# Two joined products for three in query heads 5 and 6 and in three units of the second attention's projection, and the third query tile's weight remainder made by VectorE

## What is computed

```python
def second_block(x, ...):
        xn = rmsnorm_2(h, norm1_g[layer])
        proj = xn @ w_in[layer]
        q_a, k_a, v_a, q_r, f_r, i_r, g_r = jnp.split(proj, IN_SPLITS, axis=-1)
        attn = moba_attention(q_a..., k_a..., v_a...)
        rec = hgrn2(q_r, f_r, i_r, g_r, lb_all[layer], rec_norm_g[layer])
        h = h + jnp.concatenate([attn, rec], axis=-1) @ w_out[layer]
        hn = rmsnorm_2(h, norm2_g[layer])
        h = h + peer_2(hn, ...)

def peer_2(x, wq, subkeys, u, v):
        qp = (xb @ wq).reshape(PEER_TOKEN_BLOCK, PEER_HEADS, 2, PEER_DKEY // 2)
        s = jnp.einsum('thcd,hcnd->thcn', qp, subkeys)
        v1, i1 = lax.top_k(s[:, :, 0], PEER_TOPK)
        v2, i2 = lax.top_k(s[:, :, 1], PEER_TOPK)
        ...
```

## Time and profile before

| | us |
|---|---|
| median of 3 runs | 1984.44 |
| lowest, highest | 1984.0, 1984.62 |
| the profiled execution | 1984.3 |
| its span | 1982.5 |

### The profile page before, as it was taken

One profiled execution on the slowest core, in us unless ns is written; L12 is line 12 of the kernel. 1 busy time (PEld: TensorE's weight loads), 2 busy tenths in 40 slices (PEclk: granted clock), 3 DMA queues, 4 the chain that ended last, 5 costly groups with the idle time before them and its releaser, 6 DMA issues.

```text
span 1982.5 us, 39083 instructions
## 1 busy us (share of the span) xinstructions
PE 1974.8 (100%) x13990; PEld 1766.6 (89%) x13990; DVE 1281.9 (65%) x2178; ACT 1042.3 (53%) x1361; POOL 1429.7 (72%) x606
## 2 busy tenths in 40 slices
PE   9999999999999999999999999999999999999998
PEld 9899898888888888888889899888888888888887
DVE  5256387864766899953336738886467789994333
ACT  6556545565555544445447665556555554444444
POOL 6667878888777878854448757888877787884442
PEclk9999999999999999999999999999999999999999
DMA  8444545555555555566655345555555555555653
GB/s 273 161 139 149 179 161 186 188 183 190 177 170 175 174 169 171 177 208 206 195 186 178 123 144 166 192 187 186 182 176 172 172 178 169 175 174 181 201 190 127
DMA packets 100467, 351.44 MB, mean 177 GB/s; under 512 B 12464, under 2 KB 15408, under 8 KB 100272
## 3 DMA queue, kind: packets, MB, share of 16 engines
q1 hardware_dynamic: 99680, 348.61, 53.2%
q10 hardware_dynamic: 720, 1.92, 0.3%
HBM read 349.44 MB, written 1.05 MB: 177 GB/s over the span
## 4 chain that ended last, share of the span: by engine, by line
PE 99%; DMA 0%; DVE 0%; ACT 0%; POOL 0%; SPq 0%; issue 0%
PE ps L1259 24%; PE ps L1325 12%; PE ps L1260 12%; PE ps L1327 12%; PE ps L1328 6%; PE ps L1326 6%; PE ps L732 4%; PE ps L734 4%; PE ps L733 4%; PE ps L889 4%; PE ps L1251 3%; PE ps L891 2%; PE ps L816 1%; PE ps L1235 1%; PE ps L1137 1%; PE ps L926 1%
## 5 line engine op out<-in xcount | busy, mean ns | idle before, releaser
L653 POOL TENSOR_TENSOR wlo<-ring,whi 128x1024 fp32r<-128x1024 f32 x567 | 1375.2, 2431 | 511.3 <-ACT whi L1677 425.8
L1677 ACT ACTIVATE whi<-ring 128x1024 fp32r<-128x1024 f32 x536 | 566.5, 1060 | 718.2 <-PE ps L1328 387.2
L1259 PE MATMUL ps<-hboth,whi 128*128 128x512 f32 x2048 | 714.6, 395 | 0.0
L1260 PE MATMUL ps<-hboth,wlo 128*128 128x256 f32 x2048 | 567.7, 277 | 0.0
L1259 PEld LDWEIGHTS ps<-hboth,whi 128*128 128x128 f32 x2048 | 384.1, 188 | 87.2
L1325 PE MATMUL ps<-whi,shi 128*128 128x512 f32 x1024 | 404.2, 395 | 0.0
L1327 PE MATMUL ps<-wlo,shi 128*128 128x512 f32 x1024 | 400.4, 391 | 0.0
L1260 PEld LDWEIGHTS ps<-hboth,wlo 128*128 128x128 f32 x2048 | 384.7, 188 | 0.0
L1328 PE MATMUL ps<-whi,slo 128*128 128x256 f32 x1024 | 286.7, 280 | 0.0
L1326 PE MATMUL ps<-whi,slo 128*128 128x256 f32 x1024 | 285.7, 279 | 0.0
L1327 PEld LDWEIGHTS ps<-wlo,shi 128*128 128x128 f32 x1024 | 192.2, 188 | 43.4
(11 more groups left out here) (332 smaller groups left out, 2905.2 us busy)
## 6 DMA issues: line engine op xcount, KB each, us to landing
ring<-in_weights SPq DMA_DIRECT2D x651, 512.0 KB, 3.3
act<-in_const SPq DMA_DIRECT2D x11, 198.0 KB, 4.0
act<-in_const SPq DMA_DIRECT2D x8, 192.0 KB, 4.5
xres<-in_x SPq DMA_DIRECT2D x4, 256.0 KB, 4.9
act<-in_keys ACTq DMA_DIRECT2D x1, 1024.0 KB, 4.7
ring<-in_weights SPq DMA_DIRECT2D x2, 256.0 KB, 4.8
act<-in_fgain ACTq DMA_DIRECT2D x1, 512.0 KB, 3.4
out<-act SPq DMA_DIRECT2D x1, 512.0 KB, 2.6
```

Source lines behind the costliest of these rows:

```text
L653: pool.tensor_tensor(wlo[:, j, :], ring[:, j, :], whi[:, j, :].bitcast(F32), ALU.subtract)\
L1259: pe.matmul(bank(b), whi[:, j, c], hboth[:, :, kc, :], start=kc == 0, stop=False, skip_group_check=True)
L1260: mm = pe.matmul(bank(b, 0, S), wlo[:, j, c], hhi[:, kc, :], start=False, stop=kc == KC - 1, skip_group_check=True)
L1677: eng.activation(whi[:, j, :], ring[:, j, :], ACT.Copy).then_inc(hi_ready[j], 1)
```

## The change

It has four parts.

1. `JOINED2_BANK`: units 1, 2 and 3 of the second attention's projection use `joined_columns`: two matmuls a step for three, into the banks 6 and 7, 4 and 5, 6 and 7. ACT copies the right halves to `col_part` (128 x 512), VectorE adds them to the left halves in PSUM, waits for that add, and then multiplies by the scale as before. ACT's copy stands ahead of its weight copy for the second slot of the next unit but one.
2. `JOINED_BANK`: heads 5 and 6 of both expert layers use `joined_tile` into the banks 2 and 3, 0 and 1. The high and low parts of x become one tensor, `rboth`. ACT copies the right halves to `qT`, and VectorE adds the left halves (`join_query`), once at the start of each token half of its head 2. PE's scores of these heads wait for that.
3. Head 7's two tiles go to two banks (5, then 4) and ACT copies each by itself.
4. The remainder of the third query tile moves from POOL to VectorE, which makes it after the last square and ahead of `raw_low` of the right half of x. POOL leaves it out.

```diff
+JOINED_BANK = {5: 2, 6: 0}
+JOINED2_BANK = {1: 6, 2: 4, 3: 6}
...
-                lows(at, first, range(RING))
+                query = FIRST[f"q{b}"] // RING
+                lows(at, query, range(RING))
+                lows(query, query + 1, (0, 1, 3))
+                lows(query + 1, first, range(RING))
...
+                        elif i in JOINED2_BANK:
+                            joined_columns(FIRST["in2"] + HALVES * i, JOINED2_BANK[i], None if i == 1 else [(col_copied, i - 1)] * TT)
...
+                def joined_tile(j, b):
+
+                    for kc in range(KC):
+                        c = slice(kc * P, (kc + 1) * P)
+                        pe.matmul(bank(b), whi[:, j, c], rboth[:, :, kc, :], start=kc == 0, stop=False, skip_group_check=True)
+                        mm = pe.matmul(bank(b, 0, S), wlo[:, j, c], rhi[:, kc, :], start=False, stop=kc == KC - 1,
+                                       skip_group_check=True)
+                    mm.then_inc(slot_used, 1)
+
+                def query_there(g):
+
+                    if g in JOINED_BANK:
+                        pe.wait_ge(n["q_joined"], list(JOINED_BANK).index(g) + 1)
+                    else:
+                        pe.wait_ge(n["q_copied"], g + 1 if g < min(JOINED_BANK) else g + 1 - len(JOINED_BANK))
...
+                    if h in JOINED_BANK:
+                        pe.wait_ge(xl_ready, 4 * b + 4)
+                        for c in range(2):
+                            pe.wait_ge(lo_ready[(2 * h + c) % RING], (first_q + 2 * h + c) // RING + 1)
+                            joined_tile((2 * h + c) % RING, JOINED_BANK[h] + c)
...
+                            if i in JOINED2_BANK:
+                                highs_to(FIRST["in2"] + HALVES * i + 1 + RING)
+                                eng.wait_ge(slot_used, FIRST["in2"] + HALVES * (i + 1))
+                                if i > 1:
+                                    eng.wait_ge(col_joined, i - 1)
+                                b = JOINED2_BANK[i]
+                                eng.activation(col_part, ps[:, b:b + 2, S:2 * S], ACT.Copy).then_inc(col_parted, 1)
...
+                            for c in range(2):
+                                eng.wait_ge(slot_used, first_q + 2 * h + c + 1)
+                                last = eng.activation(qT[:, h % 2, c, :], bank(5 - c, 0, S), ACT.Copy)
+                            last.then_inc(n["q_copied"], 1)
...
+                eng.wait_ge(hi_ready[2], FIRST[f"q{i + 1}"] // RING + 1)
+                eng.tensor_tensor(wlo[:, 2, :], ring[:, 2, :], whi[:, 2, :].bitcast(F32), ALU.subtract).then_inc(lo_ready[2], 1)
                 raw_low(k, 2, rlo, rhi)
                 raw_low(k, 3, rlo, rhi)
...
+                        if i in JOINED2_BANK:
+                            b = JOINED2_BANK[i]
+                            product = ps[:, b:b + 2, 0:S]
+                            eng.wait_ge(col_parted, i)
+                            eng.tensor_tensor(product, product, col_part, ALU.add).then_inc(col_joined, 1)
+                            eng.wait_ge(col_joined, i)
...
+                        if h == 2:
+                            join_query(5 + t)
```

More of the change, by code:

```diff
@@ L387, in block_program @@
         gained = flat[:, TT * D + D:TT * D + 2 * D]
+        col_part = carve(cat_at, 2, S)[0]
         late_scores = carve(LATE_SCORES, 4, TT, 2 * NKEY)[0].rearrange("p b t (c k) -> p b t c k", c=2)
-        rhi = over_at("rhi", "act", 4 * RAW_AT, [P, KC, S], F32R)
-        rlo = over_at("rlo", "act", 4 * (RAW_AT + KC * S), [P, KC, S], F32R)
+        rboth = over_at("rboth", "act", 4 * RAW_AT, [P, 2, KC, S], F32R)
+        rhi, rlo = rboth[:, 0], rboth[:, 1]
         def scores_of(h):
@@ L445, in block_program @@
         col_copied = sem("columns_copied")
+        col_parted = sem("columns_low_part_copied")
+        col_joined = sem("columns_parts_joined")
         fr_open = sem("forget_opened")
@@ L516, in block_program @@
             peer.append({n: sem(f"peer{b}_{n}") for n in (
-                "q_copied", "s_ready", "s_copied",
+                "q_copied", "q_low", "q_joined", "s_ready", "s_copied",
                 "gelu_done", "sums_ready", "exp_ready", "sel_ready", "selT_ready", "rows_ready", "eq_ready", "hot_ready",
@@ L918, in joined_columns @@
                     for t in range(TT):
-                        if half == 0:
+                        if half == 0 and free is not None:
                             pe.wait_ge(*free[t])
@@ L1220, in experts @@
                             if h >= 2 and c == 0:
-                                pe.wait_ge(n["q_copied"], h - 1)
-                            tile((2 * h + c) % RING, bank(4 + h % 2, c * S, (c + 1) * S), R, range(4 if h + c == 1 else 0, KC))
+                                pe.wait_ge(n["q_copied"], h - 1 if h < HEADS - 1 else min(JOINED_BANK))
+                            dst = bank(5 - c, 0, S) if h == HEADS - 1 else bank(4 + h % 2, c * S, (c + 1) * S)
+                            tile((2 * h + c) % RING, dst, R, range(4 if h + c == 1 else 0, KC))
                             if h + c == 1:
@@ L1226, in experts @@
                         g = h - 1
-                        pe.wait_ge(n["q_copied"], g + 1)
+                        query_there(g)
                         if g == 1:
@@ L1685, in experts @@
                     if h < HEADS:
-                        eng.wait_ge(slot_used, first_q + 2 * h + 2)
+                        if h < HEADS - 1:
+                            eng.wait_ge(slot_used, first_q + 2 * h + 2)
                         if h >= 2:
                             eng.wait_ge(n["s_ready"], h - 1)
-                        eng.activation(qT[:, h % 2, :, :], bank(4 + h % 2).rearrange("p (c t) -> p c t", c=2), ACT.Copy)\
-                           .then_inc(n["q_copied"], 1)
+                        if h in JOINED_BANK:
+                            eng.activation(qT[:, h % 2, :, :], ps[:, JOINED_BANK[h]:JOINED_BANK[h] + 2, S:2 * S], ACT.Copy)\
+                               .then_inc(n["q_low"], 1)
+                        elif h < HEADS - 1:
+                            eng.activation(qT[:, h % 2, :, :], bank(4 + h % 2).rearrange("p (c t) -> p c t", c=2), ACT.Copy)\
+                               .then_inc(n["q_copied"], 1)
+                        else:
+                            for c in range(2):
+                                eng.wait_ge(slot_used, first_q + 2 * h + c + 1)
+                                last = eng.activation(qT[:, h % 2, c, :], bank(5 - c, 0, S), ACT.Copy)
+                            last.then_inc(n["q_copied"], 1)
                         for c in range(2):
@@ L2164, in attention2 @@
                             take_scale(2)
-                        eng.wait_ge(slot_used, FIRST["in2"] + HALVES * (i + 1))
-                        eng.tensor_tensor(colT[name][:, off // P:off // P + 2, :],
-                                          bank(4 + i % 2).rearrange("p (j t) -> p j t", j=2), R, ALU.mult).then_inc(col_copied, 1)
+                        if i in JOINED2_BANK:
[4 more added lines that the diff above has]
+                            eng.wait_ge(col_joined, i)
+                        else:
+                            product = bank(4 + i % 2).rearrange("p (j t) -> p j t", j=2)
+                            eng.wait_ge(slot_used, FIRST["in2"] + HALVES * (i + 1))
+                        eng.tensor_tensor(colT[name][:, off // P:off // P + 2, :], product, R, ALU.mult).then_inc(col_copied, 1)
                     elif what == "m_values":
@@ L2276, in add_pair, with join_query @@
                     eng.tensor_tensor(a, ps[:, bb:bb + 2, 0:S], a, ALU.add).then_inc(n["u_added"], 1)
+                def join_query(h):
+                    bb = JOINED_BANK[h]
+                    eng.wait_ge(n["q_low"], list(JOINED_BANK).index(h) + 1)
+                    eng.tensor_tensor(qT[:, h % 2, :, :], ps[:, bb:bb + 2, 0:S], qT[:, h % 2, :, :], ALU.add).then_inc(n["q_joined"], 1)
                 normed(2 * b + 1)
```

2 lines of the change are left out of this document (1 added, 1 removed).

## The result

| | before | after |
|---|---|---|
| median, us | 1984.44 | 1988.61 |
| lowest to highest of 15 each | 1983.97 to 1985.73 | 1988.3 to 1988.97 |
| profiled execution's span, us | 1982.5 | 1986.9 |

The ratio after to before is 1.0021, with a 95% interval of 1.0014 to 1.0028. The forecast was 1982.8 us in a range of 1981.9 to 1984.7: the kernel is 5.8 us slower than forecast, and slower than before where it was to be faster.

What follows compares the result with a forecast made beforehand. PE was taken to bound the kernel, busy 1974.8 of 1982.5 us. From 1984.44, terms of -0.60, -0.81, -0.46 and +0.30 sum to -1.57, giving 1982.87, rounded to 1982.8 us, range 1981.9 to 1984.7.

Steps and rivals of the forecast that it cites:

- What bounds the kernel: Whole kernel: PE is busy 1974.8 of 1982.5 us, so only its own instructions or new waits can change the time.
- The slower rival: Second attention: the line misses one more POOL instruction, 4.8 us late in all; sum +2.2, 1986.6 us; chance 0.06.
- what I did not see: Anywhere in the kernel: the chance of 0.04 left for an outcome that no named case covers.
- third query tile: Both expert layers: with the remainder on VectorE, PE's wait and restart go, 2 x 0.30 = 0.60 us less.
- heads 5 and 6 joined: Expert layers' query heads: 64 steps fall from 0.3593 to 0.3467 us, 0.81 us less; 0.38 with the slower pair.
- head 7 in two banks: Scores of heads 6 and 7: an earlier second copy spares PE a restart, 2 x 0.23 = 0.46 us less.
- second attention: Joined units gain 0.29 us, but the line is 1.0 us late and PE waits 0.49 plus 0.10: net +0.30 us.
- The holds: Second attention: L2185 and the scan already waited for POOL; these waits absorb lateness, leaving 1.0 us, bounds 0.2 and 2.4.
- the rule for two inputs: Second attention: VectorE with two SBUF inputs and GpSimd exclude each other for a whole instruction, so lateness moves in whole instructions.
- a wait for POOL at unit 4: Second attention: POOL's remainders arrive ahead of PE, tightest by about 0.1 us; PE waiting there would mean the prediction is wrong.
- joined steps hardly faster: Rival on all joined places: steps stay at 0.3593 us, sum -0.60 - 0.46 + 0.30, 1983.7 us; chance 0.13.
- the formula: Joined steps: distance is columns / 2.4 plus 2.5 ns, 328 against 325 ns a step; all 112 steps save 0.3 us.

Runs made afterwards that it cites:

- 17 and 18 products: Changed kernel with 17 or 18 short products instead of 16 ahead of the experts' first stage, round 0: 1983.28 and 1983.32 us.
- the split alone: Kernel before with only head 7's two tiles in banks 5 and 4, two ScalarE copies and a wait for head 6's copy: 1989.43 us.
- 88 ns (one-step): Changed kernel with 19 short products instead of 16 ahead of the experts' first stage, round 0: 1988.02 us.
- before with 17: Kernel before with 17 short products instead of 16 ahead of the experts' first stage, round 0: 1989.68 us.
- runs with a wider last product: Changed kernel, 16 short products kept, the last 128, 256 or 384 columns wide instead of 64: 1988.55, 1988.76 and 1992.98 us.

## Why the prediction was wrong

*What bounds the kernel.* "The time can change in two ways only: PE's own instructions take less or more, or PE waits where it did not." That is true, but the first half was then applied to the changed instructions alone. **This is the step that failed.** 2048 joined steps of the experts were taken as fixed. The earlier trace rows held both distances, 0.3467 in the experts and 0.3533 in the first attention; I took the pair as bounds for the 64 steps of the heads, and did not ask why one loop body has two speeds, or whether the larger body could change. At 832 steps by 6.6 ns, 5.5 us, that question was worth more than the rest of the sum: 1982.87 + 5.5 = 1988.4, and 1988.61 was measured. The predicted sum was off as well, by 0.46 us; that the two numbers lie 0.2 apart is in part luck, since the medians differ by 0.2 us less than the profiled executions. None of the rivals was this one. The slower rival, a missed POOL instruction in the attention, did not happen; 0.04 was left for what I did not see. Which property of PE's entry picks the pattern stays open.

The terms, each from the run that does it alone:

| term | predicted | measured |
|---|---|---|
| third query tile | -0.60 | -0.57 (0.29 and 0.28) |
| heads 5 and 6 joined | -0.81 | -0.64 (0.39 less 0.07, twice) |
| head 7 in two banks | -0.46 | -0.15 (0.07 and 0.08) |
| second attention | +0.30 | +0.22 |
| sum | -1.57 | -1.14; -1.11 in the table of after |
| entry into the experts' first stage | not seen | +5.52 |

*Third tile*: right in mechanism and size. *Heads 5 and 6*: the mechanism was right, no wait for VectorE's adds appeared, and the size was off, because head 5 came in with the three-step pattern. Its 16 steps took 5.74 us (277.79 to 283.53), those of head 6 5.63; a head of three products takes 5.84, the 6.65 less the 0.81 for scores. 0.10 and 0.21, not twice 0.20.

*Head 7*: mis-sized by three. The 1.85 us of 16 scores was compared with twice 0.81. But the 0.81 of eight holds a last distance of 31 ns, since the tile behind starts so soon after it; scores stand 112 ns apart, and 16 of them take 1.79 without any wait. Only the 62 ns gap could go, and went. The split of head 7 is what turned the pattern: done alone it turned the entry of before from two to three, and taken out of the changed kernel it turned that one's from three to one. That it did so by the lost gap, and not by the other banks or the second copy, is not shown.

*Attention*: the line came 0.9 us late at the scaling, against 1.0 forecast, and PE waited at `m_turn` for 0.39 us and 0.06 more to start again, against 0.49 and 0.10. The holds took up lateness as worked out: L2185's instruction took 1.46 us instead of 2.36, the scan 2.78 instead of 4.35, and the scan ended 0.9 late. (L2185 reads one tensor of SBUF, so the rule for two inputs that the prediction quotes does not account for its hold.) The joined steps ran in the two-step pattern (16.73 us for 48, against 17.36 from unit 1's start to unit 4's in before) and gained 0.63 instead of 0.29. In unit 4 PE lost 0.42 again: 0.32 us in a wait for POOL's remainder of the second slot, which was said to arrive ahead by 0.1 us, and 0.10 in starting again. The prediction had named a wait for POOL at unit 4 as a sign of being wrong, and it came. So that the net of +0.22 is near +0.30 is partly luck: 0.34 more gain and this loss of 0.42, neither of them in the sum, nearly cancel. The rival "joined steps hardly faster" falls: 0.36 fell to 0.347 or 0.353 wherever products were joined. The Trainium skill (TensorE: Matmul & The Clock Gate, section "Back-to-back issue gap") gives the formula that the prediction set beside this rival for an isolated matmul only, and says that in a stream the weight loads set the spacing too; no run here shows steps of its 325 ns.

## What to carry to other kernels

Before summing up the touched places, look whether the same instruction sequence stands at two distances anywhere in the trace, and price the larger loop at both. When a change is slower than its own places can explain, cut the timeline at fixed instructions and compare the stages that were *not* changed. A short filler product ahead of a long run of unequal matmuls is a cheap experiment: 29 ns moved this kernel by 5.3 us, and it must be tried again after each change ahead of that run.

## What the runs showed of the hardware

Pairs of a 512-column and a 256-column product on fresh weights repeat in three stable patterns, of 346 to 347 ns, of 344 and 350, and of 350, 361 and 349. A pattern held for the 416 steps of rounds 0 to 12, through loops and semaphore waits that were already met. The three-step one also came back behind each of the 16 interruptions by gates in layer 1 of three kernels (608 steps in all), while in layer 2 of two of them the first gates turned it. Three-product steps of 256 columns stood at 120 ns a product in all kernels. The experts' second stage consists of pairs of the same widths, with other code (L1325 to L1328 in before), and none of its pairs ran slowly: their starts stood 346.7 ns apart on average in all 18 kernels, and in layer 1 the stage, up to the next layer, took 370.14 to 370.16 us. So not every run of such pairs is open to this loss, and no run here shows why this one isn't. What stands ahead goes with the pattern: the split of head 7 with its lost gap of 62 ns, one product of 29 ns more, or another pattern ahead of the twelve transposes. Both layers of a kernel came in alike in rounds 0 to 12.

Which property picks it stays open. The wait alone is out (17 and 18 products), the count of products alone is out (before against the split alone, same matmuls, two and three steps), and a simple scale of time would have to set 88 ns (one-step) and 91 ns (before with 17, three-step) apart. The runs with a wider last product were meant to hold the count and move the time; two did not move it, and the third moved it by some 50 ns, kept the pattern of rounds 0 to 12 and changed the one behind the middle, from two to three steps in layer 1 and from one to two in layer 2. At the middle, then, the place in the same pattern at which PE arrived seems to be enough, with the count held; only this run speaks for it.
